# Rotary cache keys of the samples gathered in turned form from a host layout, in four 1 KB-row gathers per half sequence

## The reference, cut to what matters

```
past_lat = cache_lat[j, page_table].reshape(B, -1, 256)     # values and 256 of the key's 320 numbers
past_pe  = cache_pe[j, page_table].reshape(B, -1, 64)       # the rotary part of the keys
s = (einsum('bthc,bsc->bhts', q_lat, kv_lat) + einsum('bthr,bsr->bhts', q_pe, k_pe)) * ATTN_SCALE
p = softmax(s, axis=-1)
o_lat = einsum('bhts,bsc->bthc', p, kv_lat)
```

## Time and profile before

| | us |
|---|---|
| median of three executions | 2508.56 |
| span of the profiled execution, first to last instruction | 2501.3 |
| median less this span | 7.3 |
| busy: PE / DVE / ACT / POOL | 2409.7 / 1686.3 / 955.5 / 227.0 |
| stretch of the samples' attention (about 1566 to 1680): DVE busy | 100.3 of 114.0 |
| the same stretch: PE busy | 86.4 of 114.0 |

### The profile page before, as it was taken

The page is one execution under the profiler, slowest core; times in us unless marked ns, Lnnn a source line. Parts: engine busy times, 40 slices in busy tenths (PEclk is TensorE's granted clock), DMA queues, the critical chain, the costliest instruction groups (busy, mean ns, idle before and its releaser), DMA issues. The chain is left out here.

```text
span 2501.3 us, 44960 instructions
## 1 busy us (share of the span) xinstructions
PE 2409.7 (96%) x18990; PEld 2284.8 (91%) x18990; DVE 1686.3 (67%) x2619; ACT 955.5 (38%) x1668; POOL 227.0 (9%) x315
## 2 busy tenths in 40 slices
PE   7999999999999999999999999789999999999999
PEld 5888999989999999999985888569989999999999
DVE  6422236797777777687455766976897777778673
ACT  4211114543333334554433666024543333334542
POOL 1000000001111110000001100210001111110000
PEclk8999999999999999999999999899999999999999
DMA  9677333237776747676010031982337776747664
GB/s 353 218 276 259 101 99 122 102 123 159 192 177 168 168 155 250 196 221 214 20 34 22 20 148 60 360 286 109 102 123 158 192 183 170 168 152 260 198 191 142
DMA packets 347203, 415.92 MB, mean 166 GB/s; under 512 B 16811, under 2 KB 290179, under 8 KB 334918
## 3 DMA queue, kind: packets, MB, share of 16 engines
q0 software_dynamic: 53904, 211.83, 28.0%
q1 hardware_dynamic: 293098, 201.20, 26.1%
HBM read 358.56 MB, written 118.08 MB: 191 GB/s over the span
## 5 line engine op out<-in xcount | busy, mean ns | idle before, releaser
L2855 PE MATMUL ps<-h_hi,w_hi 128*128 128x344 f32 x816 | 263.8, 323 | 0.8 <-ACT a_sb L1490 0.8
L2857 PE MATMUL ps<-h_hi,w_lo 128*128 128x344 f32 x816 | 260.4, 319 | 0.0
L2856 PE MATMUL ps<-h_lo,w_hi 128*128 128x344 f32 x816 | 260.3, 319 | 0.0
L1805 DVE TENSOR_TENSOR d_lo<-d_raw,d_hi 128x768 fp32r<-128x768 f32 (+2 forms) x176 | 154.0, 887 | 86.9 <-ACT d_hi L1197 86.3
L1197 ACT ACTIVATE d_hi<-d_raw 128x768 fp32r<-128x768 f32 (+2 forms) x176 | 136.2, 788 | 154.2 <-DMA d_raw<-in_ffn_w_out 82.4
L1537 ACT ACTIVATE op_hi_Y<-op_raw_Y 128x512 fp32r<-128x512 f32 x80 | 50.5, 632 | 311.8 <-DVE op_raw_Y L2359 162.0
L2855 PEld LDWEIGHTS ps<-h_hi,w_hi 128*128 128x128 f32 x816 | 153.4, 188 | 5.4 <-issue 4.3
L2857 PEld LDWEIGHTS ps<-h_hi,w_lo 128*128 128x128 f32 x816 | 153.3, 188 | 0.0
L2856 PEld LDWEIGHTS ps<-h_lo,w_hi 128*128 128x128 f32 x816 | 153.2, 188 | 0.0
L1007 POOL DMA_DIRECT2D act_d<-g_sb x52 | 41.3, 794 | 1026.3 <-DVE g_sb L2389 656.0
L3144 PE MATMUL ps<-h_hi,op_hi_X 128*128 128x258 f32 x640 | 129.7, 284 | 2.4 <-DVE op_lo_X L2340 2.4
(11 more groups left out here) (526 smaller groups left out, 7183.8 us busy)
## 6 DMA issues: line engine op xcount, KB each, us to landing
wsum_d<-in_ffn_w_out POOLq DMA_DIRECT2D x88, 704.0 KB, 11.1
mod_late<-in_mod_w SPq DMA_DIRECT2D x40, 1024.0 KB, 10.1
fr<-in_ffn_w_in SPq DMA_DIRECT2D x80, 512.0 KB, 5.2
d_raw<-in_ffn_w_out SPq DMA_DIRECT2D x72, 384.0 KB, 3.6
act_d<-g_sb POOLq DMA_DIRECT2D x52, 516.0 KB, 6.0
xc<-x_d POOLq DMA_DIRECT2D x10, 1376.0 KB, 7.0
w_raw<-in_sc_w_in SPq DMA_DIRECT2D x24, 512.0 KB, 3.7
d_raw<-wsum_d SPq DMA_DIRECT2D x32, 384.0 KB, 3.3
```

The source lines that it names most:

```text
L1805: dve.tensor_tensor(w_lo[k.slot][:, 0:k.kt, :], w_raw[k.slot][:, 0:k.kt, :], w_hi[k.slot][:, 0:k.kt, :].bitcast(F32), ALU.subtract).then_i ...
L2855: pe.matmul(o, w_hi[k.slot][:, t, :], h_hi[:, t, up_cols(c)], start=t == 0, stop=False)
L2856: pe.matmul(o, w_hi[k.slot][:, t, :], h_lo[:, t, up_cols(c)], start=False, stop=False)
L2857: ins = pe.matmul(o, w_lo[k.slot][:, t, :], h_hi[:, t, up_cols(c)], start=False, stop=t == KD - 1)
```

## The change

The host lays the rotary cache out anew (turned_pages): for each page 32 rows of 1 KB, row r holding numbers r and 32 + r of all 128 keys of the page. It also lays the page table out so that one plain DMA (page_rows) brings all indices. In place of one gather of 128 rows of 4 KB, a half sequence takes four gathers of 128 rows of 1 KB: gather q puts on partition p the row p % 32 of page 4 (p // 32) + q of the half, so that the numbers of the key stand on the partitions at once. DVE no longer turns the rotary part; the 8 rotary score matmuls of each half sequence read kr directly and write their 128 columns in permuted order. kr has 6 buffers; the wait on kt_d before a gather is gone, and DVE waits for five transfers of a half sequence instead of two. PE waits for de_ready before kt_d instead of after it. The order of the work on PE is the same.

```
-            def gather(m):
-                if m >= 5:
-                    pool.wait_ge(kt_d, m - 4)
-                for dst, table in ((pg[m % 6], lat_rows), (pgr[m % 5], pe_rows)):
-                    pool.indirect_dma_start(dst[:].rearrange("p a c -> p (a c)"), None, table,
-                                            bass.IndirectOffsetOnAxis(ap=rows16[:, m:m + 1], axis=0)
+            def gather(m):
+                pool.indirect_dma_start(pg[m % 6][:].rearrange("p a c -> p (a c)"), None, lat_rows,
+                                        bass.IndirectOffsetOnAxis(ap=rows16[:, m:m + 1], axis=0)
+                                        ).then_inc(pg_in[m % 6], 16)
+                for q in range(4):
+                    pool.indirect_dma_start(kr[m % 6][:, q].rearrange("p j t s -> p (j t s)"), None, cache_pe,
+                                            bass.IndirectOffsetOnAxis(ap=rows64[:, 4 * m + q:4 * m + q + 1], axis=0)
                                             ).then_inc(pg_in[m % 6], 16)
...
             def keys_turn(m, among=None):
 
                 s, z, n = m % 6, m % 2, HALF // 2
-                dve.wait_ge(pg_in[s], 32 * (m // 6 + 1))
+                dve.wait_ge(pg_in[s], 80 * (m // 6 + 1))
                 wait(dve, sc_mm, m - 1)
                 dve.transpose(kT[z][:, 0:n].rearrange("p t c -> p (t c)"), pg[s][:, 0:n].rearrange("p t c -> p (t c)"))
-                if among == 0:
-                    decode_top(among)
-                dve.transpose(kTr[z][:].rearrange("p t c -> p (t c)"), pgr[m % 5][:].rearrange("p t c -> p (t c)"))
-                if among:
+                if among is not None:
                     decode_top(among)
...
             def decode_scores(m):
                 b, z = m // 2, m % 2
+                wait(pe, de_ready, b - 1)
                 pe.wait_ge(kt_d, m + 1)
-                wait(pe, de_ready, b - 1)
                 for j in range(KB):
                     for g in range(4):
                         o = score_bank(b)[32 * g:32 * g + 32, z * P:(z + 1) * P]
-                        ins = pe.matmul(o, q_bd[:, j, b].rearrange("p a h -> p (a h)"), keys(m, j)[:, 4 * g:4 * g + 4, :],
+                        if j >= KR // 32:
+                            o = o.rearrange("p (t q s) -> p q t s", t=4, q=4)
+                        ins = pe.matmul(o, q_bd[:, j, b].rearrange("p a h -> p (a h)"), keys(m, j, g),
                                         start=z == 0 and j == 0, stop=j == KB - 1, skip_group_check=True)
...
-            for t in range(8):
-                pool.dma_start(rows16[t * 16:(t + 1) * 16, :], page_table.rearrange("b (h j) -> j (b h)", j=16),
-                               allow_slow_non_contiguous=True
-                               ).then_inc(ptab_in, 16)
-            pool.iota(part8[:], [[0, 1]], base=0, channel_multiplier=1).then_inc(rows_ready, 1)
...
+            pool.dma_start(page_rows[:], page_tab).then_inc(ptab_in, 16)
...
-            dve.wait_ge(rows_ready, 1)
-            dve.tensor_scalar(part8[:], part8[:], 4, None, ALU.arith_shift_right).then_inc(rows_ready, 1)
...
-            pool.wait_ge(kt_d, 2 * NS)
             load_act(2, 0)
...
+def turned_pages(cache):
+
+    n = cache.shape[0]
+    k = cache.reshape(n, 8, 16, 2, 32)
+    return np.ascontiguousarray(k.transpose(0, 4, 3, 2, 1).reshape(n * 32, 2 * PAGE))
```

More of the change, by code:

```diff
@@ L169, in build @@
 def build(nc, ins, outs):
-    (x_prompt, x_sample, cache_lat, cache_pe, page_table, mod_w, sc_w_in, sc_w_out, w_qa, w_qb, w_kva, w_kvb, w_o,
+    (x_prompt, x_sample, cache_lat, cache_pe, page_tab, mod_w, sc_w_in, sc_w_out, w_qa, w_qb, w_kva, w_kvb, w_o,
      ffn_w_in, ffn_w_out, rope_tab, lanes, vectors, states) = ins
@@ L280, in build @@
     t_var, t_root, t_inv = root_t[0:RB, 0, :], root_t[0:RB, 1, :], root_t[0:RB, 2, :]
-    rows16 = small("rows16", [P, 2 * NS], I32)
-    part8 = small("part8", [P, 1], I32)
+    page_rows = small("page_rows", [P, 10 * NS + 2], I32)
+    rows16, rows64, row_no = page_rows[:, 0:2 * NS], page_rows[:, 2 * NS:10 * NS], page_rows[:, 10 * NS:10 * NS + 2]
     csT = small("csT", [P, KD, MLANES])
@@ L401, in build @@
     pg = [at(f"pg{i}", [P, HALF, KR], o) for i, o in enumerate(slots_pg)]
-    pgr = [at(f"pgr{i}", [P, HALF, DR], A_MA + i * HALF * DR * 4) for i in range(5)]
+    kr = [at(f"kr{i}", [P, 4, 2, HALF, 8], A_MA + u * HALF * DR * 4) for i, u in enumerate((1, 2, 3, 0, 4, 5))]
     KB = (KR + DR) // 32
-    KTB = HALF * (KR + DR) * 4
+    KTB = HALF * KR * 4
     q_end = A_MA + H * T4 + 2 * TP * 4 + KC * T4 + T4
@@ L407, in build @@
     kT_at = [q_end - KB * NS * P - KTB, A_MW]
-    assert kT_at[0] >= A_MA + 5 * HALF * DR * 4 and q_end - KB * NS * P >= A_MA + H * T4 + 2 * TP * 4
+    assert kT_at[0] >= A_MA + 6 * HALF * DR * 4 and q_end - KB * NS * P >= A_MA + H * T4 + 2 * TP * 4
     kT = [at(f"kT{i}", [P, HALF, KR], o) for i, o in enumerate(kT_at)]
-    kTr = [at(f"kTr{i}", [P, HALF, DR], o + HALF * KR * 4) for i, o in enumerate(kT_at)]
     off = A_MW + KTB
@@ L573, in value_bank, with keys @@
             return bank(6 + b % 2)
-        def keys(m, j):
-            z = m % 2
+        def keys(m, j, g):
             if j < KR // 32:
-                return kT[z][:, :, 32 * j:32 * j + 32]
-            j -= KR // 32
-            return kTr[z][:, :, 32 * j:32 * j + 32]
+                return kT[m % 2][:, 4 * g:4 * g + 4, 32 * j:32 * j + 32]
+            return kr[m % 6][:, :, j - KR // 32, 4 * g:4 * g + 4, :]
         def mod_tile(j):
@@ L1078, in _ @@
                 pool.dma_start(x_d[c], xT[:, :, up_cols(c)]).then_inc(x_saved, 16)
-            for t in range(8):
-                pool.dma_start(rows16[t * 16:(t + 1) * 16, :], page_table.rearrange("b (h j) -> j (b h)", j=16),
-                               allow_slow_non_contiguous=True
-                               ).then_inc(ptab_in, 16)
-            pool.iota(part8[:], [[0, 1]], base=0, channel_multiplier=1).then_inc(rows_ready, 1)
[L1084 to L1087, removed]
+            pool.dma_start(page_rows[:], page_tab).then_inc(ptab_in, 16)
+            pool.wait_ge(ptab_in, 16)
+            pool.tensor_scalar(rows16, rows16, 8, None, ALU.mult).then_inc(rows_ready, 1)
+            pool.tensor_scalar(rows64, rows64, 32, None, ALU.mult).then_inc(rows_ready, 1)
+            pool.wait_ge(rows_ready, 2)
+            pool.tensor_tensor(rows16, rows16, row_no[:, 0:1].to_broadcast([P, 2 * NS]), ALU.add
+                               ).then_inc(rows_ready, 1)
+            pool.tensor_tensor(rows64, rows64, row_no[:, 1:2].to_broadcast([P, 8 * NS]), ALU.add
                                ).then_inc(rows_ready, 1)
@@ L1119, in _ @@
             lat_rows = cache_lat.rearrange("a (s i) c -> (a s) (i c)", s=8)
-            pe_rows = cache_pe.rearrange("a (s i) c -> (a s) (i c)", s=8)
             def gather(m):
-                if m >= 5:
-                    pool.wait_ge(kt_d, m - 4)
-                for dst, table in ((pg[m % 6], lat_rows), (pgr[m % 5], pe_rows)):
-                    pool.indirect_dma_start(dst[:].rearrange("p a c -> p (a c)"), None, table,
-                                            bass.IndirectOffsetOnAxis(ap=rows16[:, m:m + 1], axis=0)
+                pool.indirect_dma_start(pg[m % 6][:].rearrange("p a c -> p (a c)"), None, lat_rows,
[4 more added lines that the diff above has]
+                                            bass.IndirectOffsetOnAxis(ap=rows64[:, 4 * m + q:4 * m + q + 1], axis=0)
                                             ).then_inc(pg_in[m % 6], 16)
@@ L3495, in rope_table, with page_rows @@
     return np.ascontiguousarray(np.concatenate([cos, cos, -sin, sin]).astype(np.float32))
+def page_rows(table):
+    p, pages = np.arange(P, dtype=np.int32), np.asarray(table, dtype=np.int32).reshape(2 * NS, 16)
+    by_row = pages[:, p // 8].T
+    by_key = pages.reshape(2 * NS, 4, 4)[:, p // 32].transpose(1, 0, 2).reshape(P, 8 * NS)
+    return np.ascontiguousarray(np.concatenate([by_row, by_key, np.stack([p % 8, p % 32], axis=1)], axis=1).astype(np.int32))
+def turned_pages(cache):
+    n = cache.shape[0]
+    k = cache.reshape(n, 8, 16, 2, 32)
+    return np.ascontiguousarray(k.transpose(0, 4, 3, 2, 1).reshape(n * 32, 2 * PAGE))
 def vector_rows(inputs):
@@ L3536 @@
             a = a[:, 0]
+        if name == "cache_k_rope":
+            a = turned_pages(a)
+        elif name == "page_table":
+            a = page_rows(a)
         arrays[f"in_{name}"] = a
```

## The result

| kernel | median us | runs | ratio to before, 95% |
|---|---|---|---|
| before | 2511.26 | 4 (2505.52 to 2515.30) | 1 |
| after | 2557.93 | 4 (2553.47 to 2564.48) | 1.0195 [1.018, 1.0209] |

A forecast was written before the change was run, and what follows sets the result against it. DVE's 12.28 us round was taken as the bound, DMA (share 1.01) just below. Last half sequence 10.1 us earlier, 0.6 taken off for PE's clock: -9.5, span 2491.8, plus 7.3 gives 2499.1 us; range 2494.5 to 2509.

The forecast's parts named there:

- What comes on POOL: Samples' attention: five gathers take POOL 6.35 us per half sequence, 12.7 per round; POOL has the time but becomes a floor.
- DVE's round: Samples' attention: one sample's chain on DVE, 12.28 us, could fall to 10.4; about 13 expected once gathers bound it.
- Rival A: Samples' attention: PE becomes the limit at 12.6 us per round, 2503 us, or the start brings less; chance 0.32.
- Its other half: Start of the samples' stage keeps half its loss: gather 6 at 1584, -7 us, 2501.5; within the same 0.32 chance.
- The DMA stream as the next bound: Gathers of the samples' stage: DMA share near 1 from 1582 to 1649, ten half sequences at 6.6 us, 66 in all.
- The term of 512 packets at 47 ns: Gather stream: rotary rows as 512 packets of 1 KB at 47 ns raise a half sequence from 6.4 to 6.55 us.
- The start: Entry to samples' attention: head stores meet less traffic, last head output 2 us earlier, gather 6 at 1581, 5.3 earlier.
- Nothing charged for permuted columns and swapped waits: PE's rotary scores: half-rate column writes, 0.9 us per round, would be hidden; swapped waits change nothing; 0 charged.
- Rival B: Gather queue from gather 6 on: small gathers cost more than their bytes, kernel slower, 2516.5 us at 105 ns; chance 0.08.
- far case: Gather queue: each small gather holds it 1.7 us, 11.9 per half sequence, 119 in all, +52, 2561 us; chance 0.02.
- break-even: Gather stream from gather 6 on: no gain or loss at 7.6 us per half sequence, 80 ns per 1 KB packet.
- The page's rule: Trainium skill: fixed 2.0 us per gpsimd transfer plus bytes at 436 GB/s; without overlap, some 85 us slower.

The follow-up runs named there:

- e4: Kernel before, layout and turns untouched, with each half sequence's 4 KB rotary rows fetched by four gathers of 1 KB rows: 2570.3 us, ratio 1.024.
- e5: Changed kernel with the four rotary gathers per half sequence replaced by plain GpSimd copies of consecutive 1 KB rows (wrong keys): 2504.2 us, ratio 0.999.
- e1: Changed kernel with one rotary gather of 128 rows of 4 KB per half sequence instead of four of 1 KB (wrong keys): 2506.6 us, ratio 0.9987.
- e6: Changed kernel with the four rotary gathers replaced by plain copies of 1 KB rows issued by SyncE on its own queue (wrong keys): 2509.7 us, ratio 1.0006.
- e12: Changed kernel with nine gathers per half sequence, the latents and eight rotary ones of 128 rows of 512 bytes (wrong keys): 2655.4 us, ratio 1.0579.
- e3: Changed kernel with four rotary gathers per half sequence, each of 32 partitions with rows of 4 KB (wrong keys): 2569.8 us, ratio 1.0244.
- e11: Changed kernel, still five gathers per half sequence, but rotary ones unlike: one of 3.6 KB rows, three of 128-byte rows (wrong keys): 2567.3 us, ratio 1.0224.
- e9: Changed kernel with three gathers per half sequence (latents, two of 2 KB rotary rows), set apart from half sequence 6 on: 2514.1 us, ratio 1.0026.

## Why the prediction was wrong, step by step

- **The step that failed: "What comes on POOL".** It counted five gathers as 6.35 us of POOL's own time and concluded that "POOL has the time". Both are true in the trace (1.25 apart, idle between bursts), but the price falls on PE, DVE and ACT. e4 alone puts it at 60 us by ratio for 48 gathers, 1.25 each. A cue was in the earlier trace rows: PE idle for 2.72 us with "issue", from 1631.3 on, when a pair of gathers ran. I priced only the clock after it, without asking what stood beside it on POOL. It was a cue and no proof: e5 has such a stall of 3.2 us too, from 1604.2 on, when its single gather and the four plain loads had been issued.
- **DVE's round.** The turns are gone, but from gather 6 on a round took 21 to 23 us and not 13. e1 prices their removal apart from the gathers: 0.13%, some 3 us [0.3, 6], of 18 us of DVE's work. So DVE, which the prediction called the first bound, held back next to nothing by itself. Rival A named PE as the limit, and that was not it either: in e1 PE is busy 45 of 60 us in 1588:1648. Its other half, a smaller gain at the start, is what e1 shows (gather 6 at 1583.4, near the 1584 named there), but with 3 us won and not 7. Without the failed step the forecast of 2499.1 would still have been missed by some 7 us, though its range up to 2509 would have held; the kernels with one or two gathers lie at 2504 to 2510.
- **The DMA stream as the next bound.** In the change it wasn't: its share is 0.66 over the stage, and DVE's first turn waits 33.8 us for PE, not for pages. In e1 it was, as the prediction had the two bounds: share 0.98, and the stream of gathers 6 to 15 ends at 1654.0 against 1656.2, close to the 3 us that e1 gained. It took 69 us there and began at 1585.0, where the prediction had 66 from 1581. The term of 512 packets at 47 ns was wrong too, by 0.2 us per half sequence (6.55 against 6.36 as before). Queue 0 in 1580:1680 (packets, MB, share), before and then after:

```profile
q0 software_dynamic: 3370, 29.01, 72.6%
```

```profile
q0 software_dynamic: 2901, 22.40, 59.7%
```

  With 512 packets of 1 KB beside 128 of 16 KB the mean would be 4.1 KB; it is 7.7 KB, and was 8.6. In 1580:1640 the change's packets on this queue have 16384 or 4096 bytes (and 4), as before, and none has 1 KB: the rows of 1 KB travelled joined. Where packets of 1 KB do occur, in e6 on SyncE's queue, they take 48 ns each on the mean.
- **The start.** Expected: the last head output 2 us earlier, gather 6 at 1581. Measured: gather 6 at 1599.18, and s_now at 1579.1 against 1570.2. The store waits did not decide; gathers 0 to 2 had already cost the prompt's attention about 9 us (1579.1 less 1570.2, with the "remote" waits above). That 15 gathers in a row fall into another stage was not in the working at all.
- **Nothing charged for permuted columns and swapped waits.** Right: e1 has both and loses nothing.
- **Rival B** named the right side, at 0.08, and its far case (2561, by 1.7 us per small gather in the DMA queue) is near 2557.9 by number only: its mechanism, the DMA queue, is refuted by e5, which puts as many bytes in packets of the same sizes on the same queue, and by e6, which puts them on SyncE's queue in packets of 1 KB. The sum was also wrong: by the terms of the break-even beside it, a stream of 119 us ends 43 us late and not 52 (1582.3 + 119 + 0.7 + 4.4 - 1663.5), which is 2551.
- **The page's rule.** The fixed 2.0 us per transfer on the gpsimd path (the Trainium skill, DMA: Bandwidth & Descriptors, anatomy of one DMA) pointed to slower, with an estimated +85 us. By that rule e5, with as many transfers from GpSimd as the change, should have lost as well; it lost nothing. The trace does not agree with it as a price in a stream.

What stays open is the mechanism itself. That PE runs some 50 recorded matmuls at full pace and then six per 0.73 us looks like a stock of instructions that is not refilled in time; so does the prompt's attention, where few and long instructions run and eight gathers in a row pass without a loss. The Trainium skill (Runtime: NRT & Kernel Launch, instruction fetch mechanics) says that engines fetch instructions through a DMA queue of their own, in blocks, hidden behind the issue pace; if that is what the gathers delay, then not by data traffic, since e5 and e6 have the same bytes. No run here shows it, and one view leaves room for doubt. The DMA queues of the change in 1599.18:1605.2, the burst above, have one packet of kind "instruction" (packets, MB, share):

```profile
q8 instruction: 1, 0.02, 1.3%
```

1.3% of 16 engines over 6.02 us is 1.3 us; the one of the kernel before in 1599:1605.2 took 1.0. PE went on at six matmuls per 0.73 us after this packet (it started at 1600.26), and in e12 no such packet moved from 1590.77 to 1613 at all. So a block under way isn't slow; which engine it serves, and what keeps PE waiting, the profile doesn't say. Nor is it shown why e3 and e11 cost some 10 us more than the change at the same number of gathers.

## What to carry to other kernels

Count indexed gathers by how many follow each other, not by bytes, and price them on every engine that works meanwhile: here two per half sequence were free, beside a DMA stream that was the bound anyway, and each further one cost 1.1 to 1.5 us. Bursts cost time even in another stage, there only after eight in a row. A layout that needs more gathers per tile must save more than that on the engine that truly bounds; before counting such savings, check that the busy engine's gain arrives (here 3 of 18 us, because the DMA engines were full as well). An "issue" stall without a releaser should be read beside what the other engines do at that moment.

## What the hardware showed that was not expected

- An indexed gather over 128 partitions takes GpSimd 0.95 us and 0.30 between two, for rows of 128 bytes to 16 KB (0.85 over 32 partitions, in e3); four plain DMAs of 128 x 1 KB took it 2.18 us together, and the kernel lost nothing by them (ratio 0.999).
- During a burst of gathers PE got six recorded matmuls per 0.73 us, in the longer ones of e12 one in 0.7 to 3.5 us; ACT and DVE stood for "remote" signals up to 6.1 us in the prompt's attention beside 15 gathers in a row, and up to 14.7 us beside 27.
- Pauses of 0.8 to 1.1 us between the first and the other two gathers removed most of the price in the samples' stage (e9).
- With gathers of 16 KB and 4 KB rows in turn, the 16 DMA engines stayed at a share of 0.97 to 0.99 for 60 us, and this, more than VectorE at 54.86 of 60 us, held the stage of the kernels with one or two gathers.
